# Four gaps between tensors in SBUF, and weights' rings 64 bytes up, in a hybrid attention and FFN block

## The reference, cut to what matters

```python
h = rms_norm(x, pre_mix_norm[l])
proj = h @ w_in[l]
...
merged = (g[:, :, 0] * (y_a @ w_branch_a[l])
          + g[:, :, 1] * (y_b @ w_branch_b[l])
          + g[:, :, 2] * (y_c @ w_branch_c[l]))
x = x + rms_norm(merged @ w_out[l], post_mix_norm[l])
h2 = rms_norm(x, pre_ffn_norm[l])
gate, up = jnp.split(h2 @ w_ffn_in[l], 2, axis=-1)
x = x + rms_norm((jax.nn.silu(gate) * up) @ w_ffn_out[l], post_ffn_norm[l])
```

## Time and profile before

| | |
|---|---|
| median of 3 runs | 473.43 us (471.71 to 473.58) |
| the profiled execution | 471.89 us |
| its span | 470.1 us |
| PE busy | 461.3 us, 98% of the span, 2716 matmuls |
| DVE busy, ACT busy | 297.5 us (63%), 246.5 us (52%) |
| L1320, share of the chain that ended last | 79.9% |
| DMA | 85.59 MB, mean 182 GB/s |

### The profile page before, as it was taken

How to read it: one execution, slowest core, us unless ns; L and a number is a source line. 1 busy time by engine, 2 the same in 40 slices (tenths; PEclk the granted TensorE clock), 3 DMA queues, 4 the chain that set the end, 5 groups by cost and what they waited for, 6 DMA issues and landing times.

```text
span 470.1 us, 6779 instructions
## 1 busy us (share of the span) xinstructions
PE 461.3 (98%) x2716; PEld 389.5 (83%) x2716; DVE 297.5 (63%) x377; ACT 246.5 (52%) x354; POOL 53.3 (11%) x46
## 2 busy tenths in 40 slices
PE   7999999999999999999999999999999999999995
PEld 6799798997888888888888888888888888888883
DVE  5657699898627846576449786764646465553532
ACT  4958369437575955536443453762626363443510
POOL 0531012357630100000000000000000000000000
PEclk9999999999999999999999999999999999999998
DMA  8986655445443554668666555656555656666202
GB/s 296 404 264 204 194 177 169 150 137 175 141 132 110 159 169 139 186 183 314 199 198 183 175 173 167 209 177 206 182 185 181 183 179 200 221 192 188 91 0 90
DMA packets 25875, 85.59 MB, mean 182 GB/s; under 512 B 3155, under 2 KB 4852, under 8 KB 25844
## 3 DMA queue, kind: packets, MB, share of 16 engines
q1 hardware_dynamic: 24888, 84.26, 56.4%
q10 hardware_dynamic: 956, 0.90, 0.6%
HBM read 83.91 MB, written 1.25 MB: 181 GB/s over the span
## 4 chain that ended last, share of the span: by engine, by line
PE 97%; DMA 1%; DVE 1%; ACT 0%; DVEq 0%; ACTq 0%; issue 0%
PE bank L1320 80%; PE bank L1314 7%; PE bank L1346 3%; PE bank L1454 1%; DMA cols<-cols_in 1%; PE bank L1467 1%; PE bank L1495 1%; PE bank L1438 1%; PE bank L1418 1%; PE bank L1409 1%; PE bank L1468 0%; PE bank L1499 0%; DVE mo L1168 0%; PE bank L1553 0%; PE bank L1554 0%; PE bank L1551 0%
## 5 line engine op out<-in xcount | busy, mean ns | idle before, releaser
L757 DVE TENSOR_TENSOR wl<-raw,wh 128x1024 fp32r<-128x1024 f32 (+2 forms) x152 | 188.1, 1270 | 67.1 <-ACT wh L449 66.5
L449 ACT ACTIVATE wh<-raw 128x1024 fp32r<-128x1024 f32 (+2 forms) x152 | 154.0, 1045 | 67.9 <-PE bank L1320 58.9
L1320 PE MATMUL bank<-wh,hTh 128*128 128x512 f32 (+1 forms) x384 | 151.1, 393 | 1.1 <-DVE hTl L777 1.1
L1320 PE MATMUL bank<-wh,hTl 128*128 128x512 f32 (+1 forms) x384 | 148.5, 387 | 0.0
L1320 PE MATMUL bank<-wl,hTh 128*128 128x512 f32 (+1 forms) x384 | 148.4, 386 | 0.0
L1320 PEld LDWEIGHTS bank<-wh,hTh 128*128 128x128 f32 x384 | 72.1, 188 | 16.2 <-DVE hTl L777 1.5
L1320 PEld LDWEIGHTS bank<-wh,hTl 128*128 128x128 f32 x384 | 72.1, 188 | 14.6
L1320 PEld LDWEIGHTS bank<-wl,hTh 128*128 128x128 f32 x384 | 72.2, 188 | 13.5
L1246 POOL TENSOR_TENSOR st<-st 128x1 f32<-128x1 f32 x4 | 2.2, 546 | 289.1 <-DVE st L1159 171.1
L1320 PE MATMUL bank<-wh,fTh 128*128 128x512 f32 x88 | 34.7, 395 | 0.0
L1320 PE MATMUL bank<-wh,fTl 128*128 128x512 f32 x88 | 34.5, 392 | 0.0
(11 more groups left out here) (201 smaller groups left out, 534.1 us busy)
## 6 DMA issues: line engine op xcount, KB each, us to landing
raw<-w_stream SPq DMA_DIRECT2D x148, 512.0 KB, 3.6
raw<-w_stream SPq DMA_DIRECT2D x4, 328.0 KB, 8.5
x<-x_in SPq DMA_DIRECT2D x4, 256.0 KB, 5.6
bias<-bias_scratch SPq DMA_DIRECT2D x8, 128.0 KB, 4.6
x<-x_in SPq DMA_DIRECT2D x1, 1024.0 KB, 5.8
out<-mo SPq DMA_DIRECT2D x3, 256.0 KB, 2.1
post<-post_mix ACTq DMA_DIRECT2D x1, 512.0 KB, 7.1
fg<-pre_ffn SPq DMA_DIRECT2D x1, 512.0 KB, 6.8
```

The costliest lines, as they stand in the source:

```text
L449: did(act.activation(wh[:, u % SPLIT, a:2 * w], raw[:, u % RING, a:2 * w], ACT.Copy), high_done, u + 1)
L757: did(dve.tensor_tensor(wl[:, u % RING, a:2 * w], raw[:, u % RING, a:2 * w], wh[:, u % SPLIT, a:2 * w].bitcast(F32), ALU.subtract), low_do ...
L1320: ins = pe.matmul(bank[bk][:, 0:w], lhs[:, kt, t * P:(t + 1) * P], rhs[:, k], start=first, stop=final)
```

## The change

It adds a helper that allocates a tensor which nothing uses, and calls it at five places: 64 bytes ahead of the weights' rings, 448 ahead of `hTh`, 352 ahead of `yh`, 64 ahead of `mTh` and 416 ahead of `fTh`. Everything behind a gap moves up by it. No instruction is changed, and the order on each engine is the same.

```diff
--- before.py
+++ after.py
@@ -174,11 +174,18 @@
             return ctx.enter_context(nc.semaphore(name))
 
 
+        def gap(nbytes, stack=ctx):
+
+            gaps.append(sb(f"gap{len(gaps)}", [P, nbytes // 4], stack=stack))
+
+        gaps = []
+        gap(64)
         ring = ExitStack()
         raw = sb("raw", [P, RING, 1024], stack=ring)
         ring.close()
         wl = sb("wl", [P, RING, 1024], F32R)
         wh = sb("wh", [P, SPLIT, 1024], F32R)
+        gap(448)
         hTh = sb("hTh", [P, KT, S], F32R)
         hTl = sb("hTl", [P, KT, S], F32R)
         eye = sb("eye", [P, P])
@@ -187,6 +194,7 @@
         post = sb("post", [P, D])
         tmp = sb("tmp", [P, 2, 512])
         sig = sb("sig", [P, 3, TT, 512])
+        gap(352)
         yh = [sb(f"yh{b}", [P, H, S], F32R) for b in range(3)]
         yl = [sb(f"yl{b}", [P, H, S], F32R) for b in range(3)]
 
@@ -239,12 +247,14 @@
 
         wf, pw = (fg[:, k].rearrange("p t n -> p (t n)") for k in range(2))
         merging = ExitStack()
+        gap(64, merging)
         mTh = sb("mTh", [P, KT, S], F32R, stack=merging)
         mTl = sb("mTl", [P, KT, S], F32R, stack=merging)
         merged = sb("merged", [P, TT, D], stack=merging)
         h2 = sb("h2", [P, TT, D], stack=merging)
         mow = sb("mow", [P, TT, D], stack=merging)
         merging.close()
+        gap(416, late)
         fT_h = sb("fTh", [P, FT, S], F32R, stack=late)
         fT_l = sb("fTl", [P, FT, S], F32R, stack=late)
         late.close()
```

## The result

The changed kernel takes 474.78 us (median of 6, 474.68 to 474.84) against 472.03 us (median of 6 runs of the kernel before, 471.71 to 473.58). The ratio is 1.0049, 95% interval 1.0033 to 1.0066. The forecast was 468.8 us, 1% faster. Some executions of nearly every kernel here take 1.5 us longer than the others, of the kernel before those of 473.43 and 473.58 us against 471.71 to 472.09, and the 473.43 us from which the forecast started is one of them.

What follows compares the result with a forecast made beforehand. It took PE to bound the kernel, matmul count times pitch; group terms together saved 4.6 us, 471.89 becoming 467.3, and 1.5 us for the median of runs gave 468.8 us. Range 458 to 477.5 us, the forecast's own 466 to 471.

Steps and rivals of the forecast that it cites:

- What bounds the kernel: Whole kernel: PE is 97% of the chain, so time is the number of matmuls times their start-to-start pitch.
- What moves: Only addresses move; stationary minus moving start, modulo 512, is constant per group, and this distance affects the pitch.
- Rival 1: Matmul pitches: nothing moves, as earlier differences come from something other than distance; 472.5 to 474.5 us, chance 0.27.
- the sum: All matmul groups: savings and losses read from straight lines between measured distances, together 4.6 us or 1.0% saved.
- f: 264 matmuls with stationary fTh or fTl, distance 192 to 384: excess 15.7 to 8.9 ns, saving 1.8 us.
- hT: 1152 matmuls with stationary hTh or hTl, distance 0 to 448: excess 13.3 to 11.1 ns, saving 2.5 us.
- y: 156 matmuls with stationary yh or yl, distance 192 to 480: excess to 12.2 ns, saving 0.5 us.
- m: 96 matmuls with stationary mTh or mTl, distance 192 to 32: excess to 13.7 ns, saving 0.2 us.
- L1314: 288 matmuls, 256 wide, moving hTh or hTl, stationary weights, distance 0 to 64: losing 0.2 us.
- L1409: 24 matmuls, 256 wide, moving latent, stationary weights, distance 320 to 32: excess 6.7 to 13.7 ns, losing 0.2 us.
- bound of 450.1 us: Best case for all groups: every excess falls to the transposes' 2.1 ns, saving 23.3 us.
- Rival 3: Slower: hT at 448 costs what 192 costs f, +2.8 us for its 1152; ends at 477.1 us, chance 0.23.

Runs made afterwards that it cites:

- first two experiments: Changed kernel with other gaps: only 64 bytes ahead of the rings, 472.1 us, ratio 0.9994; only 448 ahead of hTh plus 64 ahead of yh, 472.78 us, ratio 1.0009.
- narrow runs: Products with yh, mTh and fTh stream only 256 of 512 moving columns, at two sets of distances; 429.14 and 432.44 us, one run each.

## Why the prediction was wrong

**What bounds the kernel** held: PE is 97% of the chain before and after, the clock stayed full, and the time followed the pitches. **What moves** held in its core: the distance matters, and a common step of 64 bytes does not, as the first two experiments show. Rival 1, no effect, is out. It was the case to which the Trainium skill's rule of two independent read ports ("TensorE: Matmul & The Clock Gate", "Step-by-step: what each phase is for") led. The runs show up to 6.7 ns per matmul between two distances, so on the time the measurement goes against that reading of it.

**The step that failed** is the sum, "straight lines between the nearest points" with "6.7 at 320" as one of them. Three things in it were wrong:

- The point at 320 came from 256 wide products, and I put it on one curve with the 512 wide ones because both widths agree on 13.3 ns at distance 0. The narrow runs show the two curves reversed: f has 120.0 ns at 0 and 113.5 at 64 with 256 columns, and 226.9 and 233.4 (at 320) with 512.
- The circle is 256 bytes, not 512. 448 is therefore 192, whose pitch of 229.0 ns stood in the trace of before; with that alone hT's term would have been a loss of 2.3 x 1152 = 2.7 us (measured 2.1) instead of a saving of 2.5. The 1152 hold 48 matmuls of 328 columns, which stayed at 149.2 to 151.2 ns at every distance; half of them stood at 224 before, which is none of the new distances, contrary to what the prediction says.
- The curve is no straight line: 226.7, 233.3, 232.4 and 229.0 ns at 0, 64, 128 and 192. f at 384 is at 128, 232.4 instead of the forecast 222.2.

Term by term, forecast against measured: hT -2.5 and +2.1 us; f -1.8 and +0.9; y -0.5 and +0.7; m -0.2 and +0.4; L1314 +0.2 and -1.4; L1409 +0.2 and +0.1. Only the last sign is right, and L1314's is wrong for the same reason as the others: 64 is 320 on the circle of 256, where the trace had 113.3 ns. Apart from the sum, the base was high: the 1.5 us put on top of the profiled execution brought it to 473.43 us, and the kernel before measured 472.03.

The bound of 450.1 us took 106.7 ns as the full rate of the transposes. That is two cycles for each of their 128 columns; at one cycle a column it would be 53.3 ns. No run shows which is theirs, so their excess of 2.1 ns is not shown either. No 512 wide group had a mean pitch below 226.7 ns in any kernel.

**Rival 3** named the right outcome: hT at 448 costs what 192 costs f, "+2.8 us for its 1152" against 2.1 measured. It put this as an "if" and had no reason for it; the period of 256 bytes is the reason. In the rest it was off, and its total loss of 3.7 us is near the measured 2.75 in part by luck, as two misses offset each other: it left y, m and f unchanged (they lost 1.9) and let L1314 lose 0.7 (it gained 1.4). Its aside that 32 past a multiple of 64 could cost something is what y and m showed; that it is an added line is not shown.

**What stays open** is the mechanism. The excess hardly changes with the loaded columns. With the width it stays the same only at distance 0 (13.3 ns at 256 and at 512 columns); at 64 it is 6.7 ns at 256 and 20.0 at 512, so a fixed cost per matmul doesn't explain it. No run tells which of the two reads waits, or whether one does.

## What to carry to other kernels

Where matmuls run back to back and PE is the whole chain, the offset between the two operands' starts is worth up to 3% of a 512 wide fp32r matmul. Measure the pitch per group, from starts, at the four multiples of 64 within 256 bytes, and keep the starts of both operands on multiples of 64. Don't carry a value from one width to another, and don't fill a map between measured points: a gap adds no instruction, and one kernel can try four distances at once. Where one tensor serves in both roles, move the weights' place per unit rather than the tensor. The prize here was small, 2.3 us of 472, because the largest group stood at the best distance already.

## What the runs showed of the hardware

- The mean pitch of fp32r matmuls of 128 x 128 by 512 depends on (stationary minus moving) modulo 256: 226.7 ns at 0, 233.3 at 64, 232.4 at 128, 229.0 at 192. At 256 columns it is 120.0 at 0, 118.6 at 128 and 118 at 192; at 64 it is 113.3 or 118, unit by unit. At 328 columns it was 149.2 to 151.2 whatever the distance.
- With the stationary tile 32 past a multiple of 64 and the weights on one, it is 233.3 ns at 512 columns, whether at distance 224, 480 or 32.
- A weight load of 64 columns takes 134 ns and one of 128 takes 188, and the pitch above them is the same to 0.7 ns.
